# Seven quarter products in the dense down projections, and the experts' tokens read as rows, in a two-block transformer kernel

## The reference

```python
def _swiglu(h, w_gate, w_up, w_down):
    return (jax.nn.silu(h @ w_gate) * (h @ w_up)) @ w_down
...
    top_v, top_i = lax.top_k(logits, TOP_K)
    top_w = jax.nn.softmax(top_v, axis=-1)
    gates = jnp.sum(jax.nn.one_hot(top_i, N_EXPERTS, dtype=jnp.float32) * top_w[..., None], axis=-2)
    out = jnp.zeros_like(x)
    for e in range(N_EXPERTS):
        out = out + gates[..., e:e + 1].astype(x.dtype) * swiglu(x, w_gate[e], w_up[e], w_down[e])
```

## Time and profile before

| | |
|---|---|
| median of 3 runs | 3351.29 us (3350.37 to 3353.44) |
| profiled execution, span from first to last instruction | 3350.1 us |
| TensorE matmul busy | 3109.3 us, 93% |
| VectorE, ScalarE, GpSimd busy | 824.6, 414.9, 333.9 us |
| mean granted TensorE clock | 0.963 of full speed |
| DMA | 609.13 MB, 182 GB/s over the span |

### The profile page before, as it was taken

The page is one execution under the profiler, slowest core; times in us unless marked ns, Lnnn a source line. Parts: engine busy times, 40 slices in busy tenths (PEclk is TensorE's granted clock), DMA queues, the critical chain, the costliest instruction groups (busy, mean ns, idle before and its releaser), DMA issues.

```text
span 3350.1 us, 41616 instructions
## 1 busy us (share of the span) xinstructions
PE 3109.3 (93%) x18128; PEld 1771.3 (53%) x18128; DVE 824.6 (25%) x1612; ACT 414.9 (12%) x1028; POOL 333.9 (10%) x376
## 2 busy tenths in 40 slices
PE   6988789999989999899988999978999999999997
PEld 2456544444447777577656776454444444444443
DVE  1136942000035776500132000253000000000002
ACT  1024111000022122200021000131000000000001
POOL 1122720000002333200000000000000000000030
PEclk8989988999999999999999999978999999999998
DMA  8670001212122112143332334214899999999992
GB/s 340 251 270 2 1 1 63 113 63 107 38 54 68 51 45 76 59 181 134 139 136 113 132 149 165 91 51 193 341 406 359 362 389 377 358 361 407 360 380 89
DMA packets 210612, 609.13 MB, mean 182 GB/s; under 512 B 6076, under 2 KB 53404, under 8 KB 203904
## 3 DMA queue, kind: packets, MB, share of 16 engines
q1 hardware_dynamic: 204912, 592.20, 46.4%
q0 software_dynamic: 5056, 13.67, 1.2%
q10 hardware_dynamic: 464, 0.60, 0.1%
HBM read 600.28 MB, written 6.16 MB: 181 GB/s over the span
## 4 chain that ended last, share of the span: by engine, by line
PE 80%; DVE 10%; issue 3%; ACT 3%; DMA 2%; another core or an unknown queue 1%; POOL 0%; POOLq 0%; ACTq 0%; DVEq 0%; SPq 0%
PE ps_ffn_gate L610 10%; PE ps_ffn_up L610 10%; PE ps_ffn_down L646 10%; PE ps_moe_down L3019 6%; PE ps_moe_gate L2974 5%; PE ps_moe_up L2974 5%; PE ps_odd L1928 4%; PE ps_lin L1408 4%; PE ps_project L528 3%; PE ps_moe_down L3025 3%; PE ps_moe_gate L2979 3%; PE ps_moe_up L2979 3%; PE ps_lin L296 3%; PE ps_ple_gate L2601 2%; DVE rec_qd L2187 2%
## 5 line engine op out<-in xcount | busy, mean ns | idle before, releaser
L610 PE MATMUL ps_ffn_gate<-hT,ring_buf 128*128 128x256 f32 (+1 forms) x1152 | 342.8, 451 | 4.3 <-issue 2.4
L610 PE MATMUL ps_ffn_up<-hT,ring_buf 128*128 128x256 f32 (+1 forms) x1152 | 336.7, 445 | 1.3
L646 PE MATMUL ps_ffn_down<-ring_buf,ffn_hiddenT 128*128 128x512 f32 x752 | 325.9, 593 | 3.0 <-issue 3.0
L610 PEld LDWEIGHTS ps_ffn_gate<-hT,ring_buf 128*128 128x128 f32 x1152 | 221.4, 193 | 120.3 <-issue 99.0
L610 PEld LDWEIGHTS ps_ffn_up<-hT,ring_buf 128*128 128x128 f32 x1152 | 217.9, 190 | 110.3 <-issue 90.0
L1928 PE MATMUL ps_odd<-ring_buf,hT 128*128 128x256 f32 (+2 forms) x1024 | 236.1, 385 | 8.1 <-ACT hg_kT L2063 6.4
L646 PEld LDWEIGHTS ps_ffn_down<-ring_buf,ffn_hiddenT 128*128 128x128 f32 x752 | 141.7, 190 | 182.0 <-issue 181.9
L695 DVE TENSOR_TENSOR ffn_hiddenT<-ffn_silu_buf,ps_ffn_up 128x256 f32<-128x256 f32 (+1 forms) x72 | 36.2, 503 | 726.1 <-PE ps_ffn_up L610 726.1
L3151 DVE TENSOR_TENSOR moe_hidden_buf<-moe_silu_buf,ps_moe_up 128x768 f32<-128x768 f32 (+1 forms) x32 | 27.3, 855 | 747.0 <-PE ps_moe_up L2979 726.4
L1928 PEld LDWEIGHTS ps_odd<-ring_buf,hT 128*128 128x128 f32 x1024 | 173.7, 192 | 55.2 <-ACT hg_kT L2063 7.9
L2974 PE MATMUL ps_moe_up<-ring_buf,moe_xg_buf 128*64 128x512 f32 (+1 forms) x1024 | 199.5, 542 | 0.1
(11 more groups left out here) (512 smaller groups left out, 3547.1 us busy)
## 6 DMA issues: line engine op xcount, KB each, us to landing
ring_buf<-in_w_exp_up_dram SPq DMA_DIRECT2D x24, 4096.0 KB, 16.6
ring_buf<-in_w_exp_down_dram SPq DMA_DIRECT2D x24, 4096.0 KB, 16.1
moe_third<-in_w_exp_gate_dram SPq DMA_DIRECT2D x16, 4096.0 KB, 17.7
mod_pieces<-in_mod_w_dram SPq DMA_DIRECT2D x40, 1024.0 KB, 6.3
ring_buf<-in_w_exp_gate_dram SPq DMA_DIRECT2D x8, 4096.0 KB, 17.5
ring_buf<-in_odd_w_in_dram SPq DMA_DIRECT2D x40, 512.0 KB, 5.4
moe_third<-in_w_exp_gate_dram SPq DMA_DIRECT2D x8, 2048.0 KB, 10.9
ring_buf<-in_w_exp_up_dram SPq DMA_DIRECT2D x8, 2048.0 KB, 7.8
```

The lines of the kernel that those rows point to most:

```text
L610: mm = nc.tensor.matmul(ps[:, 0:wide], view[:, k, i * P:(i + 1) * P], hT[:, k, first_col:first_col + wide], start=k == 0, stop=k == KD - 1)
L646: mm = nc.tensor.matmul(ps_y[i % 2][:, h, :], hidT[:, b, i * P:(i + 1) * P], view[:, b, h * 512:(h + 1) * 512], start=first, stop=end)
```

## The change

In `feed_forward` all chunks but the last make their down product by Strassen's scheme (the Winograd form): hidden values and weights are split in four quarters each (half of the tiles by half of the blocks; half of the blocks by 512 columns), and seven products of quarters are made in place of eight. VectorE makes four sums of hidden quarters and four of weight quarters, and ten adds or copies from PSUM into `Y` and a shared buffer, which is added three times in the last chunk. The last chunk goes by tiles as before, but is always added to `Y` by VectorE; no FFN keeps its sums in PSUM. FFN 1 now has chunks of 768, 768, 768 and 512, FFN 2 of 512 and three of 768, FFN 3 of 512 and four of 768.

In `experts` GpSimd scatters each token's row to the two places in a new DRAM tensor `moe_inputs` where its experts' passes read. ScalarE fetches the 96 rows of a pass by DMA, one pass ahead, and TensorE turns them by eight transposes in place of the 16 pick products. The first pass still gathers by picks. ScalarE waits for the whole scatter ahead of the first pass. `clear_rows` also clears the 15 pieces of `moe_inputs`. ScalarE's loads now go three at a time, where none had more than three; some buffers are shared.

```diff
+        half, wide_half = nt // 2, nt // 2 * P
         nb = [(hi - lo) // P for lo, hi in cuts]
         at = [sum(nb[:j]) for j in range(len(cuts))]
-        total, chunks, resident = sum(nb), len(cuts), nt == 2
+        total, chunks = sum(nb), len(cuts)
+        last = chunks - 1
+        sums_made = 10 * last + 3
...
+            mixed_w = sb(cx, "ffn_mixed_weights", [P, 2, max(nb) // 2, 512])
+            shared = sb(cx, "ffn_shared", [P, half, 512])
...
+            def quarter(j, x):
+                n = nb[j] // 2
+                return x[:, 0:n, 0:wide_half], x[:, n:2 * n, 0:wide_half], \
+                    x[:, 0:n, wide_half:wide], x[:, n:2 * n, wide_half:wide]
+
+            def mixed_hidden(j, which):
+                n = nb[j] // 2
+                return ring_buf[:, which, 8 * 768:8 * 768 + n * wide_half].rearrange("p (b n) -> p b n", b=n)
+
+            def weight_quarters(j):
+                n, w = nb[j] // 2, slot_view(3 * j + 2, nb[j], D)
+                return w[:, 0:n, 0:512], w[:, 0:n, 512:D], w[:, n:2 * n, 0:512], w[:, n:2 * n, 512:D]
+
+            def made_quarter(t, h):
+                return Y[:, tiles[t * half]:tiles[t * half] + half, h * 512:(h + 1) * 512]
...
+                def quarter_product(j, ps, x, w):
+                    for i in range(half):
+                        for b in range(nb[j] // 2):
+                            mm = nc.tensor.matmul(ps[:, i, :], x[:, b, i * P:(i + 1) * P], w[:, b, :],
+                                                  start=b == 0, stop=b == nb[j] // 2 - 1)
+                    mm.then_inc(S["ffn_down"].handle, 1)
+
+                def down_by_seven(j):
+                    n = nb[j] // 2
+                    x11, x12, _, x22 = quarter(j, hidT)
+                    w11, w12, w21, w22 = weight_quarters(j)
+                    t1, t2 = mixed_w[:, 0, 0:n, :], mixed_w[:, 1, 0:n, :]
+                    _, _, s3, _ = quarter(j, hidT)
+                    added = lambda m: pe.wait_ge(S["ffn_added"].handle, S["ffn_added"].at(10 * j + m))
+                    of_weights = lambda m: pe.wait_ge(S["ffn_weight_sums"].handle, S["ffn_weight_sums"].at(4 * j + m))
+                    of_hidden = lambda m: pe.wait_ge(S["ffn_hidden_sums"].handle, S["ffn_hidden_sums"].at(4 * j + m))
+                    await_item(pe, 3 * j + 2)
+                    if j == 0:
+                        seam.pe_room(pe, 0)
+                    added(0)
+                    pe.wait_ge(S["ffn_hidden"].handle, S["ffn_hidden"].at(at[j] + n))
+                    quarter_product(j, ps_y[0], x11, w11)
+                    if j == 0:
+                        seam.pe_room(pe, 1)
+                    of_hidden(2)
+                    of_weights(2)
+                    quarter_product(j, ps_y[1], mixed_hidden(j, 1), t2)
+                    added(2)
+                    quarter_product(j, ps_y[0], x12, w21)
+                    added(3)
+                    quarter_product(j, ps_y[1], mixed_hidden(j, 0), t1)
+                    added(4)
+                    of_hidden(3)
+                    of_weights(3)
+                    quarter_product(j, ps_y[0], s3, w12)
+                    added(6)
+                    of_hidden(4)
+                    quarter_product(j, ps_y[1], mixed_hidden(j, 2), w22)
+                    added(8)
+                    of_weights(4)
+                    quarter_product(j, ps_y[0], x22, w21)
+                    free_item(3 * j + 2)
...
-                        if not resident:
-                            pe.wait_ge(S["ffn_added"].handle, S["ffn_added"].at(j * nt + i - 1))
...
+                def down_by_tiles(j):
...
+                for j in range(last):
                     hidden(j)
-                    down(j)
+                    down_by_seven(j)
+                hidden(last)
+                down_by_tiles(last)
...
+                def first_weight_sum(j):
+                    w11, w12, _, _ = weight_quarters(j)
+                    await_item(dve, 3 * j + 2)
+                    nc.vector.tensor_tensor(mixed_w[:, 0, 0:nb[j] // 2, :], w12, w11, ALU.subtract)\
+                        .then_inc(S["ffn_weight_sums"].handle, 1)
+
+                def next_weight_sums(j):
+                    n = nb[j] // 2
+                    _, w12, _, w22 = weight_quarters(j)
+                    dve.wait_ge(S["ffn_weight_sums"].handle, S["ffn_weight_sums"].at(4 * j + 1))
+                    nc.vector.tensor_tensor(mixed_w[:, 1, 0:n, :], w22, mixed_w[:, 0, 0:n, :], ALU.subtract)\
+                        .then_inc(S["ffn_weight_sums"].handle, 1)
+                    nc.vector.tensor_tensor(w12, w22, w12, ALU.subtract).then_inc(S["ffn_weight_sums"].handle, 1)
+
+                def last_weight_sum(j):
+                    w21 = weight_quarters(j)[2]
+                    dve.wait_ge(S["ffn_weight_sums"].handle, S["ffn_weight_sums"].at(4 * j + 2))
+                    nc.vector.tensor_tensor(w21, w21, mixed_w[:, 1, 0:nb[j] // 2, :], ALU.subtract)\
+                        .then_inc(S["ffn_weight_sums"].handle, 1)
+
+                def hidden_sums(j):
+                    x11, x12, x21, x22 = quarter(j, hidT)
+                    made = S["ffn_hidden_sums"]
+                    s1, s2, s4 = (mixed_hidden(j, x) for x in range(3))
+                    dve.wait_ge(S["ffn_hidden"].handle, S["ffn_hidden"].at(at[j] + nb[j]))
+                    nc.vector.tensor_tensor(s1, x21, x22, ALU.add).then_inc(made.handle, 1)
+                    dve.wait_ge(made.handle, made.at(4 * j + 1))
+                    nc.vector.tensor_tensor(s2, s1, x11, ALU.subtract).then_inc(made.handle, 1)
+                    nc.vector.tensor_tensor(x21, x11, x21, ALU.subtract).then_inc(made.handle, 1)
+                    dve.wait_ge(made.handle, made.at(4 * j + 2))
+                    nc.vector.tensor_tensor(s4, x12, s2, ALU.subtract).then_inc(made.handle, 1)
+
+                def add_product(j, n, dst, ps, fresh, before):
+
+                    dve.wait_ge(S["ffn_down"].handle, S["ffn_down"].at(7 * j + n))
+                    src = ps[:, 0:half, :]
+                    if fresh:
+                        made = nc.vector.tensor_copy(dst, src)
+                    else:
+                        dve.wait_ge(S["ffn_added"].handle, S["ffn_added"].at(before))
+                        made = nc.vector.tensor_tensor(dst, dst, src, ALU.add)
+                    made.then_inc(S["ffn_added"].handle, 1)
+
+                def take_seven(j):
+                    mine, y11, y12, y21, y22 = shared[:, :, :], *(made_quarter(t, h) for t in range(2) for h in range(2))
+                    now, before = 10 * j, 10 * j - 10
+                    add_product(j, 1, mine, ps_y[0], j == 0, before + 3)
+                    add_product(j, 1, y11, ps_y[0], j == 0, before + 4)
+                    add_product(j, 2, mine, ps_y[1], False, now + 1)
+                    add_product(j, 3, y11, ps_y[0], False, now + 2)
+                    last_weight_sum(j)
+                    add_product(j, 4, y22, ps_y[1], j == 0, before + 7)
+                    add_product(j, 4, y12, ps_y[1], j == 0, before + 9)
+                    add_product(j, 5, y22, ps_y[0], False, now + 5)
+                    add_product(j, 5, y21, ps_y[0], j == 0, before + 10)
+                    add_product(j, 6, y12, ps_y[1], False, now + 6)
+                    add_product(j, 7, y21, ps_y[0], False, now + 8)
+
+                def add_shared():
+                    dve.wait_ge(S["ffn_added"].handle, S["ffn_added"].at(10 * last))
+                    for t, h in ((0, 1), (1, 0), (1, 1)):
+                        y = made_quarter(t, h)
+                        nc.vector.tensor_tensor(y, y, shared[:, :, :], ALU.add).then_inc(S["ffn_added"].handle, 1)
...
+                        if j < last and i == 1:
+                            first_weight_sum(j)
+                        if j < last and i == 2:
+                            next_weight_sums(j)
+                        if j == last and i == 0:
+                            add_shared()
+                    if j < last:
+                        hidden_sums(j)
+                        take_seven(j)
+                for i, t in enumerate(tiles):
+                    dve.wait_ge(S["ffn_down"].handle, S["ffn_down"].at(7 * last + i + 1))
+                    dve.wait_ge(S["ffn_added"].handle, S["ffn_added"].at(sums_made))
+                    nc.vector.tensor_tensor(Y[:, t, :], Y[:, t, :], flat_y[i % 2], ALU.add)\
+                        .then_inc(S["ffn_added"].handle, 1)
+                    behind(dve, i)
...
-    CUTS = [(0, 640), (640, 1408), (1408, 2048), (2048, 2816)]
+    CUTS = [[(0, 768), (768, 1536), (1536, 2304), (2304, 2816)], [(0, 512), (512, 1280), (1280, 2048), (2048, 2816)]]
...
-    CUTS2 = [(lo, lo + 896) for lo in range(0, HID2, 896)]
+    CUTS2 = [(0, 512)] + [(lo, lo + 768) for lo in range(512, HID2, 768)]
...
-                                 for p in range(EXPERTS - 1, 13)))
```

(31 more changed lines are left out.)

89 lines of the change are left out of this document (40 added, 49 removed).

## The result

The changed kernel takes 3330.57 us (median of 4: 3322.44, 3330.48, 3330.66, 3331.45) beside 3351.38 of before on the same chip: ratio 0.9935, interval 0.9923 to 0.9946. It is faster, by 20.8 us where 36 were forecast, and 0.6 us above the predicted range. In two later sets of runs it took 3326.45 (0.9929, 0.9912 to 0.9946) and 3327.08 (0.9928, 0.9911 to 0.9944). The profiled execution is the fastest of the first four, 3322.44 with a span of 3320.5, 29.6 less than the span of before; it can't by itself explain the median.

What follows compares the result with a forecast made beforehand. TensorE, over 99% busy, was taken to bound FFNs and experts, with experts' DMA 93% busy. Terms -27.9 - 10.4 + 1.5 + 0.3 + 0.7 = -35.8 from span 3350.1 gave 3314.3, with 1.2 added 3315; range 3302 to 3330.

Steps and rivals of the forecast that it cites:

- parts 1 to 3: Dense FFNs: fewer down products, VectorE's sums hidden, added chunk and tails; -27.9 us in all (-25 to -30).
- parts 4 and 5: Experts: shorter gather -10.4, last pass's late down piece +1.5, scatter before the first silu +0.3 us.
- part 6: GpSimd's clearing of 21 pieces for 6 ends at 1713 to 1718, before the meeting at 1719.16; +0.7 us (0 to 5).
- Parts 1 and 2: FFN down products: 37 fewer at 0.858 us each, -31.7; VectorE's sums keep up, late hand-overs +0.3 (0 to 1.5).
- C: FFNs: hand-overs of products 3 to 7 each wait for one more add; 24 us more, 3339; chance 0.10.
- Part 3: FFN chunks and tails: FFN 3's fifth chunk +1.1, adds before the seam +1.25 and +0.9, FFN 1's tail +0.3 us.
- Part 4: Experts' gather: third down piece's weights limit the gain to 1.3 us a pass, -10.4; last pass +1.5 (0 to 2.3).
- A: Experts: the gather pays in full, as the down load lands in 12.6 for 14.0; passes 116.6, 3304 us; chance 0.10.
- B: Experts: the gather pays nothing, writes and rows use up the slack; passes stay near 119.3, 3325 us; chance 0.12.
- E: Experts: the weight stream becomes the bound, slower than before if below 365 GB/s; 3379 us at 355; chance 0.03.
- Part 5: Experts' start: scatter done by 2344 to 2348, silu ready before the second gate product at 2350.27; +0.3 us (0 to 7).
- Rival D: Clearing holds up the meeting: 15 more issues each wait for a VectorE copy of 0.56; 8 later, 3323; chance 0.06.

Runs made afterwards that it cites:

- first trace: The changed kernel's first profiled execution: 3322.44 us, span 3320.5; median of its set 3330.57, ratio 0.9935.
- second and third trace: Profiles of the unchanged changed kernel, run again twice against before: 3326.45 us (span 3323.6) and 3327.08 us (profiled execution span 3332.0).
- the products alone: Changed kernel with pick products back and without spread, row fetches and added clearing, beside the kernel before: 3318.93 us, ratio 0.9905.

## Why the prediction came out as it did

The direction and the FFNs were right; the size failed at one term above all, and two gains were not in the sum. By the first trace, against the sum's steps:

| step | predicted | measured |
|---|---|---|
| FFNs (parts 1 to 3) | -27.9 (stages 15, 6, 7) | -29.8 (16.7, 6.4, 6.8) |
| experts (parts 4 and 5) | -8.6 | -7.7; -7.2 and -2.5 in the second and third trace |
| clearing (part 6) | +0.7 | +14.5 |
| jump out of the expert loop | not seen | -3.0 |
| opening, attention of layer 1 | none | -3.5 |
| sum | -35.8 | -29.6 |

The measured figure for the experts is from the first expert piece's issue to the end, less the 3.0 of the jump. "FFNs" holds the recurrence behind FFN 1 as well.

**Parts 1 and 2, right.** The changed kernel has 678 down records before the experts where some 680 were forecast and 752 stood before. The longest wait of TensorE within the quarter products is 0.4, and those have no releaser; none is for an add. C is refuted. The price of a product was right as well: two quarter products of FFN 1 start 5.15 apart, 12 records or 6 products, so 0.858 each.

```profile
612.03 5.31 PE L653 MATMUL ps_ffn_down<-ffn_mixed_weights,ring_buf 128*128 128x512 f32 x12
617.18 5.31 PE L653 MATMUL ps_ffn_down<-ring_buf,ffn_hiddenT 128*128 128x512 f32 x12
```

**Part 3, right** for FFN 3 (6.8 for 6.9); FFN 2 gave 6.4 for 5.8. FFN 1 gave 16.7 for 15.1, but that excess is luck of the execution. Its first gate product, which the change doesn't touch, before and in the first trace after:

```profile
524.60 10.10 PE L610 MATMUL ps_ffn_gate<-hT,ring_buf 128*128 128x512 f32 x16
```

```profile
522.02 8.52 PE L630 MATMUL ps_ffn_gate<-hT,ring_buf 128*128 128x512 f32 x16
```

Before, the granted clock is 0.50 up to 530.6; in the first trace it is 0.79 already from 524 to 526 and 1.00 from then on. The next such product takes 7.03 in both. Over the eleven traces with the seven products it took 8.5 to 8.9 in six, where FFN 1 and the recurrence gained 16.0 to 16.8, and 9.9 to 10.2 in five, where they gained 14.0 to 14.5. From that product's start to the first product of the recurrence the slower kind is 14.7 to 15.0 shorter than before, so the forecast stands.

**Part 4, right in mechanism.** The third down piece's weights limit what the shorter gather gives: TensorE waits 1.41 in the second pass, 1.56 and 1.50 in the next, for the 1.3 forecast.

```profile
2528.02 7.09 PE L3162 MATMUL ps_moe_down<-ring_buf,moe_hiddenT 128*64 128x512 f32 x32 [1.41 <-DMA ring_buf<-in_w_exp_down_dram]
```

Passes are 118.2 to 118.9 in the first trace where 118.0 was said: the gate pieces of most passes are 0.2 to 1.0 late. The prediction had asked only whether the next up piece would be late (a slack of 0.5) and not whether the gate piece ahead of it would. What it lacked is the price of a wait beyond its length, 1.69 by the lower clock. That is a good part of what makes the other traces worse than the first (3.4 of the 5.3 that the third loses in the experts): 120.0 for one pass in the second, 120.1 and 120.7 in the third. A, B and E fall: no pass is 116.6, those of the changed kernel are 118.5 on average and not 119.3, and the DMA engines move 379 GB/s from 2300 to 3200 where E needs less than 365.

**Part 5, right.** The row fetch is issued at 2320.13 and the first silu's turn comes on time; nothing waits for the spread.

**Part 6, the step that failed:** "Four such batches and one piece of 4 end at 1713 to 1718". One batch's 9.84, taken where only one weight load ran beside it, was multiplied by four; beside the loads that follow, the three other batches took 11.8 to 14.7. The forecast gave the whole clearing 43.4 from its first issue, inside the 45.5 after which TensorE went on before; in the trace of after TensorE goes on 58.6 after that issue. Counted from 1673.66 that is 1732, 13 behind 1719.16; by the issue times the stage is 14.5 longer, of which 0.6 is also there in the trace of the products alone. The margin of one to six us carried a risk that the range took at 0 to 5. Rival D had the right place and a wrong mechanism and price.

The errors partly cancelled in the profiled execution (3322.4, inside the range), and in the other executions not: the medians are 8 us above it in the first set and 4 to 5 in the later ones. That the first trace fell inside is luck: its clearing cost 13.8 more than forecast, and what made up for it is 3.0 of code position, 3.5 of opening and attention that no term stood for, and 1.6 of clock in FFN 1. Of what the two slower traces lose against it, the slow products, the lowered clock in two other stages and the opening explain most.

## What to carry to other kernels

A transfer on an idle queue is free only as long as nobody waits for its end: work out when the last batch lands with the batches' own waits and the weight stream beside it, and give it one transfer, or a stage with hundreds of us to spare and loads with slack (in FFN 3 all batches at once still cost 4.8, one to a chunk nothing). Where TensorE is to wait anyway, a longer single wait can cost more than its length: one of 2.0 us cost 3.7, one of 0.9 cost 0.9. And measure each part alone: here one part gave 32 (3 of them by where code stands), the other nothing, and the version with the clearing spread in FFN 3 and the transposes made twice, at 3310.5 us, is 16 below the best of the three sets of the change as it was made. Before a difference of 2 or 3 us between two traces is given to an edit, look whether a product that the edit doesn't touch took the same time in both.

## What the runs showed that was not expected

- After waits of TensorE of 1.6 to 2.6 us within dense work the granted clock fell to the lower level, and the next 32 records took 1.69 more. It is not a matter of the wait alone: behind 2.49 an up product took 8.78 in the first trace, behind 2.60 one took 7.09 in the second.
- The same work differs between executions in steps: 64 records behind the attention of layer 1 took 27.7 or 29.9, and FFN 1's first gate product 8.5 to 8.9 or 9.9 to 10.2, whichever of the kernels with the seven products ran.
- Taking 0.77 us of TensorE work out of each pass made the kernel 7.6 us slower, adding 0.77 made it no slower.
- 128 empty instructions at TensorE's start made the kernel before 3.8 us faster (the profiled spans differ by 1.6).
- 5.9 MB written as one transfer took 31.4 us beside the weight loads, and TensorE went on 32.5 after its issue; in batches of up to five 47.9 passed until then.
